# Attention of the first two layers merged with the output products of the other mixer groups

## The chip, the cores and the metric

One Trainium2 chip, one core. The metric is the device time of one launch in microseconds (us); three runs of the kernel before stand beside one profiled execution.

## The reference, cut to what matters

Four transformer layers over 256 tokens of width 1024 in float32, each modulated by a condition vector. The first two ("mix" layers) are touched by the change:

```python
def mixer_block(h, ...):
    (a_h, a_b, a_c, n_q, n_kv, n_g, l_q, l_k, l_v, l_g, l_lr, m_u, m_v) = split_cols(h @ w_in, SPLIT_SIZES)
    outs = jnp.stack([
        short_conv_mixer(a_h, a_b, a_c, conv_w),                       # group 0
        nsa_mixer(n_q, n_kv, n_g, positions, cmp_pos, cmp_w1, cmp_w2),  # group 1
        gla_mixer(l_q, l_k, l_v, l_g, l_lr, gla_gate_w2, gla_gate_b),   # group 2
        gmlp_mixer(m_u, m_v, gmlp_ws, gmlp_b),                          # group 3
    ], axis=2)
    outs = rms_norm(outs, grp_gain.reshape(N_MIXERS, GROUP_WIDTH))
    return outs.reshape(B, S, D_MODEL) @ w_o

mod = cond @ w_mod[l] + b_mod[l]
sh1, sc1, gt1, sh2, sc2, gt2 = split(mod, 6)
x = x + gt1 * rms_norm(mixer_block(rms_norm(x, g0) * (1 + sc1) + sh1, ...), g1)
x = x + gt2 * rms_norm(square(relu(h @ w_up)) @ w_down, g3)
```

Each group is 256 wide, and the norm over a group ends in one factor per token and group. `nsa_mixer` compresses keys and values (a product with `cmp_w1`), forms scores against compressed, selected and windowed keys, takes three softmaxes, and adds the three results with sigmoid gates. Layer 2 is a hybrid of a delta rule and stick-breaking attention, layer 3 retention; their arithmetic isn't touched.

## The kernel before, in words

All weights come as one stream of 1 MB slots (`pack_stream`, in the order that `plan` writes by hand) through a ring of six; the SP queue loads slot n when slot n-6 has been used (`load_weights`). A weight slot is split into a high and a low float32r part: ScalarE copies the high part (`split_hi`, L417), VectorE subtracts it (`split_lo`, L424), into two buffers used in turn. Each tile of a product is then three matmuls, high by high, low by high and high by low; a slot is 48 matmuls of 256 columns, in two halves with a semaphore each. A modulation slot isn't multiplied on TensorE: VectorE reduces it against the condition vector (`mod_sums`, L435), 4 slots for one of the 24 modulation vectors. `mods_beside` and `merge` spread these slots between the weight slots of a phase, and VectorE takes both kinds strictly in stream order.

A mix layer runs through these phases:

- `gemm_phase` ("proj", L529): 12 slots of the input product, 4 PSUM banks in turn. Each engine's program calls the next piece of a generator from `short_mixers` after each slot (`piece`), and what is left after the last (`rest`): the gated linear attention, the gated MLP and the short convolution run beside the products. The slots of the attention's inputs (q, keys, values and gates) are the last three, 9 to 11.
- `nsa_phase` (L1205 to L1457), in a block of its own, with all engines meeting before and after it: GpSimd clears the compression operand (L1239), VectorE adds positions to it (L1251) and rotates q and k (L1254 to L1264); TensorE turns q, multiplies the two compression slots (L1354), turns the rotated q and k, then computes scores (L1371, L1385), VectorE scales and masks them (L1296) and takes the row maxima, ScalarE takes the exponentials (L1451), TensorE turns the probabilities (L1410) and multiplies by the values (L1418); VectorE combines the three branches and TensorE turns the result.
- `group_norm_phase` (L1461 to L1502): squares of all four groups on ScalarE, their sums over features by a ones matrix with 512 columns (L1488), which gives the rows spread over all partitions, then Ln and Exp of [128, 1024] on ScalarE (L1476, L1482), and eight VectorE operations (L1500).
- `rows_gemm_phase` ("out", L812): 4 slots of the output product. GpSimd splits the activations into high and low parts (`split_acts`, L755 and L757). In layer 0 the 4 slots of modulation vector 4 stand between the weight slots. The last slot runs tile by tile, with sums of squares between (L601), and the norms of the next phase follow (L609, L636, L644).
- "up" and "down" of the feed-forward part.

The block of layer 0 ends its out phase with the loads of the second condition vector and of the constants of layers 2 and 3 (`later_inputs`, L2182 to L2184).

## Time and profile before

| what | us |
|---|---|
| three runs: median, lowest, highest | 1677.92, 1675.04, 5094.15 |
| profiled execution, its own time | 1681.13 |
| its span, first to last instruction | 1679.4 |
| TensorE matmul busy in it | 1529.5 |
| VectorE, ScalarE, GpSimd busy | 1106.8, 757.7, 397.8 |
| HBM read | 333.83 MB, 199 GB/s over the span |

A row of a timeline has the start and duration in us, the engine, the line of the kernel, the operation, output<-input, shapes and count; in brackets the idle time of the engine before it and what ended that. Several matmul records may be missing from a trace, so that a count can be a little short.

### The profile page before, as it was taken

Reading aid. Unit: us, or ns where it says so; the run is one execution under the profiler, and the core shown is the slowest. Engines: PE = TensorE matmul, PEld = TensorE weight load, DVE = VectorE, ACT = ScalarE, POOL = GpSimd, SP = SyncE. Lnnn points to the kernel's source line nnn. Section 1 sums busy time; section 2 is a strip of 40 time slices with the busy share of each in tenths; the row PEclk is TensorE's granted clock in tenths of the full one; section 3 lists DMA queues with packets and bytes.
Section 4 is the critical chain, followed back from the end, with each engine's and each line's share of the span. In section 5 each row is a group of like instructions: output and inputs, shape, how many; then the busy total and the mean of one; then the engine's idle time right before and its main releaser. Section 6 shows DMA issues by size and latency. Waiting matters only on the chain. (4 is left out here: it accounts for less than half of the span.)

```text
span 1679.4 us, 28072 instructions
## 1 busy us (share of the span) xinstructions
PE 1529.5 (91%) x11950; PEld 1489.0 (89%) x11950; DVE 1106.8 (66%) x1491; ACT 757.7 (45%) x1016; POOL 397.8 (24%) x369
## 2 busy tenths in 40 slices
PE   3898689999898689999899787999999998999998
PEld 3886579999887489999899687999999996999998
DVE  7874758699455549779675655777449763556554
ACT  3533445533562536543487323444335443344432
POOL 0000302099000022069200212200227800401022
PEclk7997769999799779999799897999999999989999
DMA  9760549789241127879454002577546771536550
GB/s 394 305 226 1 188 170 372 301 317 345 100 170 55 75 101 273 343 289 344 156 192 160 1 1 100 199 296 291 218 151 253 274 284 68 189 139 238 213 201 26
DMA packets 47213, 336.69 MB, mean 200 GB/s; under 512 B 5361, under 2 KB 5745, under 8 KB 6769
## 3 DMA queue, kind: packets, MB, share of 16 engines
q1 hardware_dynamic: 46224, 333.03, 53.1%
q8 instruction: 94, 1.54, 0.3%
q10 hardware_dynamic: 864, 1.87, 0.3%
q14 instruction: 31, 0.25, 0.0%
HBM read 333.83 MB, written 1.05 MB: 199 GB/s over the span
## 5 line engine op out<-in xcount | busy, mean ns | idle before, releaser
L424 DVE TENSOR_TENSOR weights_hi_lo<-ring,weights_hi_lo 128x1024 fp32r<-128x1024 f32 x426 | 554.8, 1325 | 299.1 <-ACT weights_hi_lo L417 297.9
L417 ACT ACTIVATE weights_hi_lo<-ring 128x1024 fp32r<-128x1024 f32 x426 | 445.7, 1058 | 545.9 <-PE PS L529 295.0
L529 PE MATMUL PS<-hi,weights_hi_lo 128*128 128x256 f32 x3200 | 522.8, 286 | 19.0 <-ACT hi L644 12.1
L529 PEld LDWEIGHTS PS<-hi,weights_hi_lo 128*128 128x128 f32 x3200 | 448.0, 194 | 21.5 <-issue 19.4
L812 PE MATMUL PS<-acts_hi_lo,weights_hi_lo 128*128 128x256 f32 x3552 | 437.6, 286 | 22.4 <-DVE weights_hi_lo L424 11.6
L812 PEld LDWEIGHTS PS<-acts_hi_lo,weights_hi_lo 128*128 128x128 f32 x3552 | 433.5, 193 | 26.8 <-POOL acts_hi_lo L757 14.3
L755 POOL CAST acts_hi_lo<-arena 128x256 fp32r<-128x256 f32 x148 | 133.2, 900 | 843.3 <-PE PS L812 424.6
L529 PE MATMUL PS<-lo,weights_hi_lo 128*128 128x256 f32 x1600 | 325.0, 285 | 0.0
L435 DVE CUSTOM_DVE_ANT_0 ring<-ring,cond 128x1024 f32<-128x1024 f32 x192 | 256.4, 1374 | 0.0
L529 PEld LDWEIGHTS PS<-lo,weights_hi_lo 128*128 128x128 f32 x1600 | 251.7, 193 | 0.0
L529 PE MATMUL PS<-weights_hi_lo,hi 128*128 128x256 f32 x1248 | 203.7, 285 | 3.5 <-DVE weights_hi_lo L424 2.2
L757 POOL TENSOR_TENSOR acts_hi_lo<-arena,acts_hi_lo 128x256 fp32r<-128x256 f32 x148 | 177.3, 1198 | 11.8
L529 PEld LDWEIGHTS PS<-weights_hi_lo,hi 128*128 128x128 f32 x1248 | 173.9, 191 | 5.8 <-issue 5.6
L529 PE MATMUL PS<-weights_hi_lo,lo 128*128 128x256 f32 x624 | 126.3, 284 | 0.0
L529 PEld LDWEIGHTS PS<-weights_hi_lo,lo 128*128 128x128 f32 x624 | 97.4, 190 | 0.0
L601 PEld LDWEIGHTS PS<-constS,arena 128*128 128x128 f32 x384 | 62.8, 254 | 12.3 <-ACT arena L636 11.4
L601 PE MATMUL PS<-constS,arena 128*128 128x1 f32 x384 | 63.0, 292 | 10.6 <-ACT arena L636 9.9
L1987 POOL TENSOR_TENSOR arena<-arena,constS 128x1024 f32<-128x1024 f32 x6 | 12.3, 2062 | 148.8 <-DVE arena L1915 138.8
L644 ACT ACTIVATE hi<-spare,mods 128x256 fp32r<-128x256 f32 x64 | 31.7, 506 | 32.3 <-DVE spare L655 32.3
L405 PE MATMUL PS<-constS,arena 128*128 128x128 f32 x120 | 19.7, 321 | 27.5 <-DVE arena L1336 7.6
L405 PEld LDWEIGHTS PS<-constS,arena 128*128 128x128 f32 x120 | 16.5, 167 | 30.0 <-issue 9.7
L636 ACT ACTIVATE arena<-X 128x512 f32<-128x512 f32 (+1 forms) x40 | 21.7, 545 | 43.8 <-PE PS L601 20.7
(339 smaller groups left out, 1084.5 us busy)
## 6 DMA issues: line engine op xcount, KB each, us to landing
ring<-in_stream_dram SPq DMA_DIRECT2D x313, 1024.0 KB, 4.9
constS<-in_const_dram SPq DMA_DIRECT2D x1, 1856.0 KB, 11.9
cond<-in_rows_dram SPq DMA_DIRECT2D x2, 512.0 KB, 6.0
arena<-in_x_dram ACTq DMA_DIRECT2D x1, 1024.0 KB, 12.1
smallS<-in_small_dram SPq DMA_DIRECT2D x1, 883.0 KB, 12.8
out_dram<-arena ACTq DMA_DIRECT2D x2, 256.0 KB, 2.4
out_dram<-arena SPq DMA_DIRECT2D x2, 256.0 KB, 2.8
constS<-in_const_dram SPq DMA_DIRECT2D x1, 320.0 KB, 14.1
```

What stands on the lines that cost most here:

```text
L405: mm = pe.transpose(PS[:, bank0 + i // 4, i % 4 * P:(i % 4 + 1) * P], src_of(i), ident)
L417: act.activation(wsp[:, g % 2, 0, at:at + HALF], ring[:, n % RING, at:at + HALF], ACT.Copy).then_inc(*ready.one())
L424: dve.tensor_tensor(wsp[:, g % 2, 1, at:at + HALF], ring[:, n % RING, at:at + HALF], wsp[:, g % 2, 0, at:at + HALF].bitcast(F32), ALU.subt ...
L435: ins = dve.tensor_tensor_reduce(w[:, r, :], w[:, r, :], cond[:, 0 if q < 12 else 1, :], 1.0, 0.0, ALU.mult, ALU.add, mods[:, q, k:k + 1])
L529: mm = pe.matmul(o, lhs, rhs, start=k + g + j == 0, stop=k == KD - 1 and j == 2, skip_group_check=True)
L601: mm = pe.matmul(PS[:, bank, m:m + 1], sq[:, u % 2, c * SEQ + m * P:c * SEQ + (m + 1) * P], ones[:, 0:1], start=u + c + m == 0, stop=u == ...
L636: act.activation(sq[:, u % 2, 0:len(tiles) * SEQ], X[:, tiles[0]:tiles[-1] + 1, :].rearrange("p k t -> p (k t)"), ACT.Square).then_inc(*xs ...
L644: act.activation(hi[:, k, :], tmp[:, k % 4, :], ACT.Identity, bias=mods[:, q, k:k + 1]).then_inc(*hd.one())
L755: pool.tensor_copy(asp[:, a % 2, 0, g, :], src).then_inc(*acts_hi.one())
L757: pool.tensor_tensor(asp[:, a % 2, 1, g, :], src, asp[:, a % 2, 0, g, :].bitcast(F32), ALU.subtract).then_inc(*acts_lo.one())
L812: mm = pe.matmul(y_of(k), w[:, g, k * P:(k + 1) * P], x[:, g, :], start=i + g + j == 0 and (k % 2 == 0 or k == KD - 1), stop=i == last and ...
L1987: pool.tensor_tensor(CT[v % 2], LT, cst(f"level{v}").unsqueeze(1).broadcast_to((P, 8, P)), ALU.mult).then_inc(*ctd.one())
```

## The change

1. Order of the 12 input slots: q and the keys move from places 9 and 10 to 4 and 5; mu, lg, ah, ac, ab move back to 6 to 10. The two compression slots are put into the proj phase, behind slots 4 and 5.
2. `nsa_inputs`: clearing, position adds and rotation run on GpSimd, the compression product, turning of q and of the rotated q and k on TensorE and their copies on ScalarE, all as pieces beside the proj slots (`side_by_side` calls the pieces of both generators). Proj has 3 PSUM banks in turn. The pieces of `short_mixers` stand one or two slots earlier, the convolution last.
3. `nsa_out_phase` replaces `nsa_phase` and `group_norm_phase`: phase "mixed" has three of the four output slots (groups 2, 3, 0 in that order, rows 4, 6, 0 of w_o), and the last one (group 1, the attention's) is left to "out". Score tiles rotate over banks 3 to 7; the order of scores, turns, products and sums is written by hand. The first output slot runs between the first and the second half of the turning of probabilities, the other two after the attention's products.
4. The group norms take the sum of squares with one column (`ones[:, 0:1]`) into [128, 2] per group, take the root and reciprocal of those narrow columns, and spread them by `spread_group` into PSUM; groups 2, 3 and 0 together, group 1 at the end.
5. In layer 0 the four modulation slots of vector 4 stand in the mixed phase, after the first output slot.
6. No separate blocks in layers 0 and 1. The constants of layers 2 and 3 are loaded in layer 1 (their room holds q, k and probabilities until then), behind a wait for the attention's products; the second condition vector at the end of layer 0.

```diff
-        groups = (("lk", "lr"), ("kc", "vc", "lq"), ("mv",), ("lv",), ("mu",), ("lg",), ("ah",), ("ac",), ("ab",),
-                  ("q",), ("ks", "ks", "kw", "kw"), ("vs", "vw", "ng"))
+        groups = (("lk", "lr"), ("kc", "vc", "lq"), ("mv",), ("lv",), ("q",), ("ks", "ks", "kw", "kw"), ("mu",), ("lg",),
+                  ("ah",), ("ac",), ("ab",), ("vs", "vw", "ng"))
...
+            proj[at[5] + 1:at[5] + 1] = [("cmp", ("cmp", l, 1))]
+            proj[at[4] + 1:at[4] + 1] = [("cmp", ("cmp", l, 0))]
...
+            first, others = merge(outs[:1], ("mixed", l)), [("gemm", s) for s in outs[1:3]]
+            phases.append((("mixed", l), first + [("mod", s) for q in mods_beside(("mixed", l)) for s in mod_slots(q)] + others))
+            outs = outs[3:]
...
+                gemm_phase(blk, ("proj", l), token_major, evac, banks=3, split_weights=True,
+                           beside=(side_by_side(pe, nsa_pe), side_by_side(act, nsa_act), dve, pool))
...
         # TensorE, nsa_out_phase
+                pe.wait_ge(*grc.at(1))
+                spread_group(0, 2, 0, True)
+                spread_group(1, 2, 256, False)
+                turn_probs(1)
+                pe.wait_ge(*sd.at(1))
+                turn_probs(2)
+                pe.wait_ge(*wt.at(8))
+                for g in range(2):
+                    rows_half(pe, slots[0], g, y_of, fresh=True)
...
+                attend(0, 0)
+                pe.wait_ge(*on.at(6))
+                attend(1, 2)
+                rows_half(pe, slots[1], 0, y_of, fresh=False)
+                pe.wait_ge(*fin.at(1))
+                transposes(pe, lambda i: O[:, i % 2, i // 2 * P:i // 2 * P + P], 4, 3, ft)
+                rows_half(pe, slots[1], 1, y_of, fresh=False)
+                rows_half(pe, slots[2], 0, y_of, fresh=False)
+                sums(3, 0, 0, True).then_inc(*gsum.one())
+                rows_half(pe, slots[2], 1, y_of, fresh=False)
+                pe.wait_ge(*grc.at(2))
+                spread_group(3, 2, 0, True)
...
         # VectorE, nsa_out_phase
+                normed(2, 2, 0)
+                for what, n, q, kk in todo:
+                    if what == "mod":
+                        mod_sums(dve, order, n, q, kk)
+                dve.wait_ge(*ready["gate"])
...
+                split_lo(dve, slots[1])
...
+                split_lo(dve, slots[2])
+                dve.wait_ge(*ft.at(1))
+                dve.tensor_copy(oT[:, 2:4, :], PS[:, 3, :].rearrange("p (k t) -> p k t", k=2)).then_inc(*nt.one())
+                dve.wait_ge(*grt.at(2))
+                dve.reciprocal(gr[:, 6:8], gr[:, 6:8]).then_inc(*grc.one())
                 for n in following:
                     split_lo(dve, n)
+                normed(3, 2, 0)
```

## Rows read from the trace of the kernel before

**Rows 1.** The profile's busy time, share of the span and count of TensorE.
```profile
PE 1529.5 (91%) x11950; PEld 1489.0 (89%) x11950; DVE 1106.8 (66%) x1491; ACT 757.7 (45%) x1016; POOL 397.8 (24%) x369
```

**Rows 2.** Stretches: busy us (count) of each engine, granted clock, DMA share, GB/s.
```profile
36.00:124.00 88.00, 82.60 (x636) 79.67 (x635) 69.09 (x118) 43.66 (x59) 4.47 (x6) 0.95 0.73 282
124.00:178.00 54.00, 39.20 (x229) 33.46 (x229) 26.16 (x60) 15.23 (x47) 0.95 (x1) 0.68 0.00 1
...
442.00:528.00 86.00, 81.44 (x636) 78.52 (x636) 50.76 (x83) 46.23 (x62) 4.25 (x6) 0.97 0.39 135
528.00:577.00 49.00, 33.61 (x229) 29.65 (x229) 25.98 (x60) 15.47 (x48) 0.95 (x1) 0.79 0.00 1
```

**Rows 3.** Timeline of TensorE, layer 0, from the end of proj to out.
```profile
122.73 1.04 PE L405 MATMUL PS<-constS,arena 128*128 128x128 f32 x8
127.30 1.08 PE L405 MATMUL PS<-constS,arena 128*128 128x128 f32 x4 [3.53 <-PEq L2198]
130.46 9.96 PE L1354 MATMUL PS<-ring,spare 128*32 128x128 f32 x64 [2.08 <-DVE spare L1251]
...
161.43 10.47 PE L1418 MATMUL PS<-arena 128*128 128x64 f32 x48 [0.84 <-ACT arena L1455]
...
188.83 19.73 PE L812 MATMUL PS<-acts_hi_lo,weights_hi_lo 128*128 128x256 f32 x144 [5.24 <-POOL acts_hi_lo L757]
212.19 5.46 PE L812 MATMUL PS<-acts_hi_lo,weights_hi_lo 128*128 128x256 f32 x24 [3.63 <-DVE weights_hi_lo L424]
...
223.32 1.24 PE L601 MATMUL PS<-constS,arena 128*128 128x1 f32 x8
```

**Rows 4.** The same in layer 1: end of proj, and end of out.
```profile
526.54 1.03 PE L405 MATMUL PS<-constS,arena 128*128 128x128 f32 x8
...
615.69 1.24 PE L601 MATMUL PS<-constS,arena 128*128 128x1 f32 x8
```

**Rows 5.** Timeline of TensorE in the two proj phases: where it waits.
```profile
68.78 0.71 PE L529 MATMUL PS<-weights_hi_lo,hi 128*128 128x256 f32 x4 [1.15 <-DVE weights_hi_lo L424]
...
78.74 1.19 PE L529 MATMUL PS<-hi,weights_hi_lo 128*128 128x256 f32 x4 [3.97 <-DVE weights_hi_lo L424]
...
477.03 0.72 PE L529 MATMUL PS<-weights_hi_lo,hi 128*128 128x256 f32 x4 [1.08 <-DVE weights_hi_lo L424]
484.18 0.71 PE L529 MATMUL PS<-hi,weights_hi_lo 128*128 128x256 f32 x4 [1.14 <-DVE weights_hi_lo L424]
```

**Rows 6.** The chain that ended last: a stretch of unbroken slot products.
```profile
1483.31 127.60 PE PS L529 x1056
```

**Rows 7.** Groups of TensorE in 528 to 587 us (layer 1): busy us, mean ns.
```profile
L1418 PE MATMUL PS<-arena 128*128 128x64 f32 x48 | 5.5, 275 | 0.8 <-ACT arena L1455 0.8
```

**Rows 8.** Timeline of VectorE, layer 0.
```profile
44.20 1.22 DVE L435 CUSTOM_DVE_ANT_0 ring<-ring,cond 128x1024 f32<-128x1024 f32 x1
...
67.41 2.36 DVE L424 TENSOR_TENSOR weights_hi_lo<-ring,weights_hi_lo 128x1024 fp32r<-128x1024 f32 x2
...
120.90 0.69 DVE L1096 TENSOR_TENSOR arena<-arena 128x512 f32<-128x512 f32 x1
...
124.48 0.69 DVE L1104 TENSOR_TENSOR arena<-arena 128x512 f32<-128x512 f32 x1
...
146.87 3.85 DVE L1296 SCALAR_TENSOR_TENSOR arena<-PS,constS 128x512 f32<-128x512 f32 x8
...
193.14 1.75 DVE L435 CUSTOM_DVE_ANT_0 ring<-ring,cond 128x1024 f32<-128x1024 f32 x1
```

**Rows 9.** Timeline of GpSimd, layer 0, the first split of activations in out.
```profile
187.32 0.59 POOL L755 CAST acts_hi_lo<-arena 128x256 fp32r<-128x256 f32 x1 [59.11 <-DVE arena L1500]
188.00 0.78 POOL L757 TENSOR_TENSOR acts_hi_lo<-arena,acts_hi_lo 128x256 fp32r<-128x256 f32 x1
```

**Rows 10.** Timeline of ScalarE, layer 0, in the group norm.
```profile
182.24 1.28 ACT L1476 ACT_TABLE_LOAD   x1
183.53 1.27 ACT L1476 ACTIVATE arena<-PS,constS 128x512 f32<-128x512 f32 x2
```

More of the change, by code:

```diff
@@ L92, in mods_beside @@
         return [2, 3]
-    if kind == "out" and l == 0:
+    if kind == "mixed" and l == 0:
         return [4]
@@ L458, in slots_of @@
             mod, todo, seen = mods_beside(name), [], 0
+            state["cmp"] = [n0 + d for d, (what, _) in enumerate(items) if what == "cmp"]
             for d, (what, _) in enumerate(items):
+                if what == "cmp":
+                    continue
                 if what == "mod":
@@ L499, in _ @@
                 load_weights(sp)
-                if name == ("proj", 0):
-                    sp.wait_ge(sig("layer0_inputs").sem, 32)
             @blk.tensor
@@ new lines, in side_by_side, with run, nsa_views @@
+        def side_by_side(*works):
+            def run(*args):
+                left = [w(*args) for w in works]
+                while left:
+                    left = [w for w in left if next(w, STOP) is not STOP]
+                    yield
+            return run
+        def nsa_views():
+            return {"zT": later[:, 0:1024].rearrange("p (q n) -> p q n", n=32), "hid": later[:, 1024:1152],
+                    "hidT": later[:, 1152:1184].rearrange("p (j n) -> p j n", j=2), "kcT": later[:, 1184:1200],
+                    "vc": later[:, 1200:1264], "gate": later[:, 1264:1288].rearrange("p (m c) -> p m c", m=TT),
+                    "wgt": later[:, 1288:1312].rearrange("p (b a) -> p b a", b=3), "mx": later[:, 1312:1328],
+                    "sm": later[:, 1328:1344], "sc": later[:, 1344:1472].rearrange("p (a n) -> p a n", n=16),
+                    "mxc": later[:, 1472:1480], "rsc": later[:, 1480:1488],
+                    "qT": unloaded(0, 2, SEQ), "qrT": unloaded(512, 2, SEQ), "krT": unloaded(1024, 2, SEQ),
+                    "QKR": unloaded(1536, TT, 512), "turns": unloaded(2560, 2, 64)}
@@ L974, in short_mixers @@
+        def short_mixers(l, convT, lqT, lkT, lrT, LV, LG, MU, MV, oT, blocks, rotation):
             S = 8192
@@ L1502, in group_norm_phase @@
-            state["mixed"] = [on.at(k + 1) for k in range(KD)]
+                normed(3, 2, 0)
+            state["mixed"] = [on.at(7), on.at(8)]
+            state["attended"] = ob.at(2)
             close()
@@ L2191, in _, with outputs @@
                 act.activation(cond[:, 1, :], cond[:, 1, :], ACT.Silu).then_inc(*sig("cond2_ready").one())
-            @blk.sync
-            def _(sp):
-                sp.wait_ge(sig("layer2_inputs").sem, 32)
         layers = [{"mix": mix_layer, "hyb": hyb_layer, "ret": ret_layer}[kind](l) for l, kind in enumerate(LAYERS)]
+        def outputs(blk, l, mixed, **how):
+            rows_gemm_phase(blk, ("out", l), l, mixed, 0, next_norm=(l, 1), **how)
         with block() as blk:
             start_phase(blk)
-            layers[0][0](blk)
-        for l in range(len(LAYERS)):
-            _, mixers, finish, mixed = layers[l]
-            mixers()
-            with block() as blk:
-                if finish:
-                    finish(blk)
-                rows_gemm_phase(blk, ("out", l), l, mixed, 0, acts_ready=state.pop("mixed", None), next_norm=(l, 1))
-                if l == 0:
+            for l in range(2):
+                inputs, mixers, mixed = layers[l]
+                inputs(blk)
+                mixers(blk)
+                outputs(blk, l, mixed, acts_ready=state.pop("mixed"), fresh=False)
+                if l == 1:
                     later_inputs(blk)
@@ L2212, in build, with _ @@
                     second_condition(blk)
+            layers[2][0](blk)
+            @blk.sync
+            def _(sp):
+                sp.wait_ge(sig("layer2_inputs").sem, 32)
+        for l in range(2, len(LAYERS)):
+            _, mixers, mixed = layers[l]
+            mixers()
+            with block() as blk:
+                outputs(blk, l, mixed)
+                ffn_phases(blk, l)
                 if l + 1 < len(LAYERS):
```

711 lines of the change are left out of this document (417 added, 294 removed).

## The prediction

> **What bounds the kernel now.** I read the page first: TensorE is busy 91% of the span [rows 1], so the kernel is near its bound as a whole and only stages where TensorE isn't fed can give anything. The view by stretches finds them [rows 2]. In proj TensorE is busy 82.6 of 88 us (layer 0) and 81.4 of 86 us (layer 1), at clocks of 0.95 and 0.97. Right behind, in the attention block, it is busy 39.2 of 54 and 33.6 of 49 us at 0.68 and 0.79, no other engine is half busy either, and the DMA engines move nothing: a chain of short steps between engines. The timeline of TensorE then gives its length [rows 3, 4]. In layer 0 its last work of proj ends at 122.73 + 1.04 = 123.8, the output product starts at 188.8 and ends at 223.32 + 1.24 = 224.6; three slots take 19.7 us, then it waits 3.6 us for VectorE, which had the modulation slots in between. So 100.8 us from the end of proj to the end of out. In layer 1 this stretch is 527.6 to 616.9, 89.3 us. Even in proj TensorE waits where VectorE's split is late: 1.15 + 3.97 us in layer 0 and 1.08 + 1.14 in layer 1 [rows 5], all at the places where the compression slots go now.
>
> All that isn't in these two layers stays bound by TensorE as it is; the chain that ended last shows that state: 1056 matmuls in 127.60 us, 0.121 us each, so 5.8 us for a slot of 48 and 2.9 for a half [rows 6].
>
> **Part 1, proj.** It gains the 32 compression matmuls (64 records), 4 + 8 turns of q and k and some small ones. At 1.04 us for 8 records of 128 columns [rows 3] the 64 cost 8.3 us (above, 9.96 by their own row, which was in part at the low clock; below, nothing where TensorE waits anyway). The 12 turns are 1.5, the small ones 0.9. Sum 10.7. Placed behind slots 4 and 5 they cover the waits of 5.1 and 2.2 us [rows 5]. Proj ends 5.6 us later in layer 0 and 8.5 later in layer 1. The position adds and the rotation go to GpSimd, which is busy 4.5 of the 88 us [rows 2]; at 0.8 us for an operation on 256 columns [rows 9] 17 operations are 14 us, and it has the time of four slots, 23 us, before their result is asked for: hidden. Cover gone, each microsecond of it would delay slot 11. Three banks for four: ScalarE has two slots (11.6 us) to empty a bank, where a piece of its own blocks it for about 5: nothing. The work on ScalarE and VectorE beside proj stays below their free time (44 and 69 busy of 88).
>
> **Part 2, from the end of proj to the first output product: 12.2 us.** VectorE still has the convolution, 120.90 to 125.17 before, 4.3 us [rows 8], and reaches it 1.3 us before TensorE ends because turned outputs and the next slot's split stand ahead of it: 3.0. Meanwhile TensorE does four score tiles. Then square 0.8, sums 3.3, root and reciprocal 0.7, spreading 2.4 (scores and masks stand ahead on both engines), first normed row 0.6, and GpSimd 0.59 + 0.78 = 1.4 [rows 9]. The masks go at 3.85/8 = 0.5 us each [rows 8] and end about then.
>
> **Part 3, the mixed phase.** First slot 5.8, at 18.0. Sixteen turns of probabilities, eight of compressed ones, a spread and the compressed result are some 42 records of 0.13: 5.5. The values product 5.5 by layer 1's row [rows 7], 10.5 by layer 0's [rows 3]; I take 5.5, since products have been running just before: at 29.0. In layer 1 the two last slots follow without a wait: half 2.9, turn of the result 0.6, three halves 8.7, sums and spread 1.7: at 42.9. In layer 0 VectorE has the four modulation slots from 22.1 on: 8 x 1.22 [rows 8] + 0.4, gate weights 1.4, half a split 1.2, so TensorE gets its next weights at 34.9, 5.9 us late. The result needs the other half split and five combining steps of 0.7, at 39.6; with turn, three halves, sums and spread 50.6. What is queued behind the modulation slots on VectorE is thus the whole rest of the phase. But the 3.6 us wait that they make in out today goes [rows 3].
>
> **Part 4, tail and out.** Two normed rows 1.0 and two splits on GpSimd 2.8 are on the path, at a narrow norm in place of the wide one. The last slot with its sums took 12.4 us after a wait in layer 0 (212.19 to 224.56); it is 5.8 + four sums of about 1.0 at best. I take 11.1 and 10.5. New stretch: layer 0 50.6 + 3.8 + 11.1 = 65.5, layer 1 42.9 + 3.8 + 10.5 = 57.2. Saved: 100.8 - 65.5 - 5.6 = 29.7, and 89.3 - 57.2 - 8.5 = 23.6. Sum 53.3 us.
>
> **What the sum leaves out.** It has some 25 handovers per layer without their gaps, and its values are those of a fast clock. Against that, before, the same values product took 10.5 us at one clock and 5.5 at the other, 5.0 apart [rows 3, 7]. I take 3.7 us per layer for both, 7 in all: 46 us saved. On the profiled execution's 1681.1 that is 1635; it stands 3.2 above the median of the runs, so 1677.9 - 46 = 1632 us.
>
> **The moves that cost nothing.** The 2 MB of constants go from layer 0's out phase to layer 1's; the ring is full there and TensorE-bound products follow, at a DMA share below 0.8. The wait of SP for the attention's products is long met when SP comes to it; behind it stand the up slots' loads, which would stall if it were not. The second condition vector is loaded before layer 0's last norm ends. If its landing were late, ScalarE would hold the first splits of proj 1: at most a few us once.
>
> **Two rules weighed.** ScalarE goes through a table load before Ln, and the next activation starts 1.29 us after the load began [rows 10]. The Trainium skill (ScalarE: Activation LUTs, What ACT_TABLE_LOAD costs) puts a switch at 1283 ns plus a drain of about 1380, 2.66 us; with three switches on the path of each layer (gate, root, exponential) that rule takes 8 us off the gain, 1640 for 1632. The trace agrees with the first figure and shows no drain behind the load, so the sum stays. Second: one reduction takes 1.22 us with GpSimd idle and 1.75 while GpSimd splits [rows 8]. The Trainium skill (GPSIMD Engine Reference, Key points) says that GpSimd shares its SBUF interfaces with VectorE, and the trace agrees. For the change it is two-sided: 14 us more of GpSimd beside proj, at 40% on what VectorE does then, is up to 5 us per layer of VectorE time in a stage with 19 to free, and the modulation slots run after GpSimd's last split, which is why I price them at 1.22.
>
> **Rivals.** (a) *The chain keeps its length.* Scores, softmax, turns and values are handed over as before, and the products don't fill the gaps but stand in the queue ahead of links that the chain waits for. For it: every engine's order is fixed by hand, and the first output slot stands on TensorE between turns that could run. Then only what left the chain is gained: compression and turns, 123.8 to about 142 less 10.7, some 8 us a layer with the covered waits, and about 5 for norm and meetings of the engines: 26 in all, 1652. Against it: three slots, 17 us a layer, then still run inside gaps of 15 us (54 less 39.2), so some must fit. (b) *The clock.* Slower than before if TensorE stays at 1.2 GHz from the end of proj to up. Its place: both mixed phases and the last slots. Price: small matmuls of about 22 us double, four slots go from 5.8 to 10.3 each, 40 us a layer, 80 in all; 80 - 53 = 27, so 1705. It decides against the change from two thirds of these stretches at the low level on, a granted clock of about 0.67. For it: the attention block has 0.68 today in layer 0 [rows 2]. Against it: there are products in it now, and in proj the clock is 0.95. (c) *The edit does nothing where it matters*, because other work bounds the two layers: the DMA share is 0 and no engine is full there, so I give it almost nothing; it would be 1676.
>
> **Chances.** Forecast, saved between 34 and 64: 0.76. (a) with (c): 0.18. (b): 0.06, of which 0.03 is over 2%. The range reaches down to 1613, where proj hides all compression (another 12 us beyond the sum), and up to 1660, past (a). A measurement of this kernel tells about 2% from no change. Faster by over 2% (below 1644.4): 0.77; within 2%: 0.20; slower: 0.03.
>
> **What would show it.** Right: proj grows by 4 to 9 us per layer while its waits for VectorE at slots 5 and 6 are gone; end of proj to end of out is 65 to 72 us in layer 0 and 57 to 64 in layer 1; a wait of TensorE for VectorE of about 6 us behind the values product in layer 0 and none in layer 1; a granted clock over 0.8 in both mixed phases; everything from up 0 on keeps its length. Wrong: more than 15 us between the end of proj and the first output product; a clock under 0.7; waits of proj slots for banks; position adds on GpSimd that TensorE waits for.

## The result, and the profile after

The changed kernel took 1627.6 us in the median of 4 runs (1623.3 to 1631.5), for 1677.7 of the kernel before beside it: a ratio of 0.971, with a 95% interval from 0.967 to 0.974. That is 50 us less, where 46 were forecast. One of the four runs of the kernel before took 5094.15 us; times are compared by their medians. The page of the changed kernel's profiled execution, the line of busy times as in [rows 1]:

```profile
PE 1514.1 (93%) x12038; PEld 1483.2 (91%) x12038; DVE 1083.4 (67%) x1447; ACT 748.3 (46%) x1012; POOL 420.5 (26%) x403
```

There are 88 matmul records more and 15 us less time in them: less of the work ran at the low clock (1.2 GHz of 2.4), and the granted clock over the whole span is 0.943 for 0.926. The view by stretches, columns as in [rows 2]: proj, the mixed phase and out, in layer 0 and then in layer 1.

```profile
35.00:126.00 91.00, 90.58 (x717) 87.35 (x717) 71.99 (x119) 47.30 (x69) 15.79 (x24) 0.97 0.77 302
126.00:177.00 51.00, 43.80 (x340) 41.67 (x340) 39.30 (x75) 25.73 (x58) 15.97 (x12) 0.90 0.38 142
177.00:207.00 30.00, 21.38 (x120) 20.53 (x120) 9.86 (x18) 9.12 (x22) 4.04 (x4) 0.66 0.19 70
409.00:503.00 94.00, 91.35 (x717) 87.87 (x716) 52.45 (x83) 49.06 (x70) 14.55 (x24) 0.97 0.40 147
503.00:548.00 45.00, 42.60 (x340) 40.51 (x340) 30.30 (x58) 26.02 (x58) 6.64 (x13) 0.92 0.19 70
548.00:577.00 29.00, 20.15 (x121) 19.44 (x122) 10.19 (x18) 9.64 (x22) 4.02 (x4) 0.74 0.36 142
```

The reader should see three things. Proj no longer waits in layer 0 (90.6 busy of 91 us), although it now holds the compression. The stretch behind it is busy 43.8 of 51 us at a clock of 0.90, where it was 39.2 of 54 at 0.68, and three output slots are in it. And the loss that is left stands in the third row: 21 busy of 30 us at 0.66. The timeline of TensorE tells where, the one of [rows 3] after the change:

```profile
126.20 1.65 PE L1425 MATMUL PS<-constS 64*128 64x256 f32 x16 [0.58 <-ACT arena L977]
...
137.96 5.92 PE L780 MATMUL PS<-acts_hi_lo,weights_hi_lo 128*128 128x256 f32 x48 [1.02 <-DVE heads L1587]
...
149.75 3.79 PE L1445 MATMUL PS<-arena,constS 128*128 128x64 f32 x32
153.38 1.95 PE L1445 MATMUL PS<-arena,heads 128*128 128x64 f32 x16
160.40 5.46 PE L780 MATMUL PS<-acts_hi_lo,weights_hi_lo 128*128 128x256 f32 x24 [5.07 <-DVE weights_hi_lo L432]
...
181.34 5.48 PE L836 MATMUL PS<-acts_hi_lo,weights_hi_lo 128*128 128x256 f32 x24 [4.97 <-POOL acts_hi_lo L765]
...
192.18 1.24 PE L609 MATMUL PS<-constS,arena 128*128 128x1 f32 x8
```

Proj ends at 126.20 less 0.58, 125.6; out ends at 193.4. Two long waits are left, 5.1 us for VectorE behind the values product (the product of the probabilities with the values, L1445) and 5.0 us for GpSimd ahead of the last slot, and behind each the first 24 products take 5.5 us for 3: the granted clock is 0.50 behind both waits (160.4 to 165.8 us, 181.3 to 186.6 us). In layer 1 the stretch runs from 502.8 to 563.3 with one such wait, 4.96 us ahead of the last slot, whose first 24 products take 4.5 us.

### The profile page after: what moved, and what is told of

It reads as the page before. It is cut to its first block and busy times, and to the rows that moved or that the text cites. A ratio compares the mean times of both kernels' runs of the same rounds, so it can differ in the third digit from the quotient of the medians.

```text
span 1626.1 us, 28191 instructions
## 1 busy us (share of the span) xinstructions
PE 1514.1 (93%) x12038; PEld 1483.2 (91%) x12038; DVE 1083.4 (67%) x1447; ACT 748.3 (46%) x1012; POOL 420.5 (26%) x403
## 5 line engine op out<-in xcount | busy, mean ns | idle before, releaser
L537 PEld LDWEIGHTS PS<-hi,weights_hi_lo 128*128 128x128 f32 x3200 | 445.6, 193 | 18.2 <-issue 14.9
L836 PE MATMUL PS<-acts_hi_lo,weights_hi_lo 128*128 128x256 f32 x3264 | 400.2, 285 | 18.2 <-POOL acts_hi_lo L765 9.9
L763 POOL CAST acts_hi_lo<-arena 128x256 fp32r<-128x256 f32 x148 | 139.1, 940 | 837.4 <-PE PS L836 418.4
L765 POOL TENSOR_TENSOR acts_hi_lo<-arena,acts_hi_lo 128x256 fp32r<-128x256 f32 x148 | 173.5, 1172 | 11.9
L609 PEld LDWEIGHTS PS<-constS,arena 128*128 128x128 f32 x384 | 61.3, 248 | 12.6 <-ACT arena L644 11.7
L609 PE MATMUL PS<-constS,arena 128*128 128x1 f32 x384 | 61.6, 288 | 10.7 <-ACT arena L644 9.9
L2177 POOL TENSOR_TENSOR arena<-arena,constS 128x1024 f32<-128x1024 f32 x6 | 12.3, 2063 | 151.2 <-DVE arena L2105 142.3
```

Of the source, the lines that this page charges most:

```text
L537: mm = pe.matmul(o, lhs, rhs, start=k + g + j == 0, stop=k == KD - 1 and j == 2, skip_group_check=True)
L609: mm = pe.matmul(PS[:, bank, m:m + 1], sq[:, u % 2, c * SEQ + m * P:c * SEQ + (m + 1) * P], ones[:, 0:1], start=u + c + m == 0, stop=u == ...
L763: pool.tensor_copy(asp[:, a % 2, 0, g, :], src).then_inc(*acts_hi.one())
L765: pool.tensor_tensor(asp[:, a % 2, 1, g, :], src, asp[:, a % 2, 0, g, :].bitcast(F32), ALU.subtract).then_inc(*acts_lo.one())
L836: mm = pe.matmul(y_of(k), w[:, g, k * P:(k + 1) * P], x[:, g, :], start=fresh and i + g + j == 0 and (k % 2 == 0 or k == KD - 1), stop=i = ...
L2177: pool.tensor_tensor(CT[v % 2], LT, cst(f"level{v}").unsqueeze(1).broadcast_to((P, 8, P)), ALU.mult).then_inc(*ctd.one())
```

## The experiments

All are compared with the changed kernel at 1627.6 us; each ran beside the kernel before (1678.3 to 1679.8). Four undo a part of the change, one does a part alone, and the rest move or add single pieces. Each kernel has one trace; its time is the median of four or more executions. A table behind experiment 12 sets the traces side by side.

**1. All output slots behind attention.**

```diff
         # TensorE, nsa_out_phase
-                for g in range(2):
-                    rows_half(pe, slots[0], g, y_of, fresh=True)
                 turned_taken(pe, 1)
...
-                rows_half(pe, slots[1], 0, y_of, fresh=False)
...
                 spread_group(3, 2, 0, True)
+                for i in range(3):
+                    for g in range(2):
+                        rows_half(pe, slots[i], g, y_of, fresh=i == 0)
```

> The changed kernel, with the three output slots of each mixed phase moved on TensorE behind the turn, the sums and the spread of the attention's group, so that none of them stands beside the attention; the second and third are split later too. Theory overlap (the gain is mostly products that fill gaps of the attention): 3 x 5.8 = 17.4 us a layer come back, 35 in all, about 1660 us. Theory short chain (the gain is that the attention's own tail has become short and that meetings of engines are gone; the slots only use 5 to 10 us of gaps, and without them the 5 us wait ahead of the last slot goes): 2 us more in layer 0 and 3 in layer 1, about 1633.

1629.2 us (1627.3 to 1631.3), ratio 0.970 [0.968, 0.973]: 1.5 us more than with the products among the links of the chain, which the intervals don't tell from nothing. Timeline of TensorE in layer 0:

```profile
162.20 1.12 PE L413 MATMUL PS<-constS,arena 128*128 128x128 f32 x4 [4.01 <-DVE arena L1673]
164.76 1.87 PE L1453 MATMUL PS<-constS,arena 128*128 128x1 f32 x8 [1.45 <-ACT arena L1531]
167.18 1.22 PE L1459 MATMUL PS<-constS,stat 128*128 128x128 f32 x4 [0.55 <-DVE stat L1681]
168.06 18.94 PE L780 MATMUL PS<-acts_hi_lo,weights_hi_lo 128*128 128x256 f32 x144
186.84 3.00 PE L836 MATMUL PS<-acts_hi_lo,weights_hi_lo 128*128 128x256 f32 x24
```

The chain of attention still waits (4.0 and 1.5 us), but 144 products then run without a gap, the last slot too (3.0 us for 24). From the end of proj to the end of out it is 70.9 us for 67.8 in layer 0, and 67.2 for 60.5 in layer 1, where 4.4 of the 6.7 us are the values product (10.0 us for 5.6). Out of layer 1 ends 8.6 us later than in the changed kernel. The rest of the kernel, from there on, took 1054.1 us for 1062.8 at the same instructions; the granted clock between 800 and 1100 us was 0.97 for 0.93. So the products among the links are worth some 9 us in the two layers by these two traces, 1.5 us in the time, and 35 in neither. A difference of this size between two such kernels can come from the clock in layers that no edit touches, and what a stretch says and what the time says must both be read.

**2. Compression behind proj again.**

```diff
-            proj[at[5] + 1:at[5] + 1] = [("cmp", ("cmp", l, 1))]
-            proj[at[4] + 1:at[4] + 1] = [("cmp", ("cmp", l, 0))]
+            proj += [("cmp", ("cmp", l, h)) for h in range(2)]
```

(with its products, turn and copies behind the last slot on each engine)

> The changed kernel, with both compression slots behind the twelfth proj slot and the compression, its turn and its second product behind all of proj. Theory of the prediction (the compression covers the waits of TensorE for VectorE at slots 5 and 6 in proj): these waits come back, about 5 us in layer 0 and 2 in layer 1, and behind proj stand 7.3 us that proj lost, with 3 us of hand-overs, of which VectorE's convolution covers 3: +5 and +2, at most +8 and +5: 1635 to 1641. Rival (place in proj is worth little since TensorE does the same matmuls somewhere): under 3 us in all. Rival (it was the main part): over 20 us.

1640.0 us (1638.0 to 1640.7), 12.4 more. TensorE's timeline in proj and behind it:

```profile
68.40 0.73 PE L536 MATMUL PS<-weights_hi_lo,hi 128*128 128x256 f32 x4 [1.16 <-DVE weights_hi_lo L431]
...
78.36 1.19 PE L536 MATMUL PS<-weights_hi_lo,hi 128*128 128x256 f32 x4 [3.96 <-DVE weights_hi_lo L431]
...
124.47 7.17 PE L1083 MATMUL PS<-ring,later 128*32 128x128 f32 x64
```

The waits of proj [rows 5] are back, which the compression had covered, and its 64 products stand on the path with 7.2 us, four small steps behind them. Out of layer 1 ends 13.9 us later; the values product, at the low clock in this trace, is some 5 of these in layer 1.

**3. The narrow form of the group norm alone, in the kernel before.**

```diff
-                    pe.matmul(PS[:, p, :], ones, pair[:, 2 * p:2 * p + 2, :], start=True, stop=True).then_inc(*sp_.one())
+                            mm = pe.matmul(PS[:, 0, 2 * g + m:2 * g + m + 1], sq[:, g, c, m * P:(m + 1) * P], ones[:, 0:1],
+                                           start=g + c + m == 0, stop=c == 1, skip_group_check=True)
...
+                act.activation(gr, PS[:, 0, 0:8], ACT.Sqrt, bias=cst("eps"), scale=1.0 / 256).then_inc(*grt.one())
```

> The kernel before, with only its group norm narrow: sums with one column for all four groups, one root and reciprocal of [128, 8], eight spreading matmuls, for the ones matrix with 512 columns and Ln and Exp of [128, 1024]. Theory (the narrow form alone gives little; what gives is that only one group is left behind the attention): from the last squares 0.9 sums, 0.5 root and reciprocal, 2.9 spread, 0.5 row, 1.4 split against 10.7 us from the block's start to the first product with 2.2 of squares: about 2 us less per layer, 1673 to 1677. Rival (the narrow form is a main part of the gain): over 4 us per layer, below 1669.

1678.5 us, ratio 0.999 [0.997, 1.001]: nothing. Its 16 sums with one column (32 records) took 6.98 us and the 8 spreading products (16 records) 3.42, at the low clock after a wait, and the first output product started at 190.8 us for 188.8 [rows 3].

**4. The early norms undone as well.** The kernel of experiment 1, and groups 2, 3 and 0 normed together with the attention's.

```diff
-                for i in range(3):
-                    mm = sums(i, 2, 2 * i, i == 0)
...
-                spread_group(0, 2, 0, True)
-                spread_group(1, 2, 256, False)
...
+                for i in range(4):
+                    mm = sums(i, 0, 2 * i, i == 0)
...
+                spread_group(2, 3, 0, True)
+                spread_group(3, 3, 256, False)
```

> All output slots behind attention's norm, as in the run that took 1629.2 us, and also the norms of groups 2, 3 and 0 not before the attention's but together with it. If the early norms of three groups are what shortened the way from the turned result to the first product (13.1 us before, 5.9 in the run with the products last): plus 6 to 8 us per layer, 1641 to 1645 us. If the wide form of the norm and the meetings of all engines were the cost: 1630 to 1634.

1641.4 us (1640.0 to 1641.9), 12.2 more than experiment 1. From the turn of the result to the first output product it is 12.3 us for 5.9 in layer 0. But in the two traces the stretches from the end of proj to the end of out grew by 1.4 us in layer 0 and 5.0 in layer 1, out of layer 1 ends 8.1 us later, and another 5.7 us lie behind it, at the same instructions. So of the norm it is the place that pays and not its form; how much per layer is open between 4 us by the traces and 6 by the time.

**5. The rotation behind proj.**

```diff
             def rotation(pool, order):
-                pool.wait_ge(*taken.at(6))
+                pool.wait_ge(*taken.at(12))
```

(with the turns of the rotated rows and their copies behind proj)

> The changed kernel with the rotation of q and k on GpSimd, the turning of the rotated rows and their two copies moved from beside the proj slots to behind them. GpSimd takes 2.02 us for the copy and 12 steps of 0.40, 7 us, then 8 turns of 1.3 and a copy of 0.6 ahead of the first scores. If the chain of attention sets the end: plus 8 to 10 us per layer, 1644 to 1648 us. If the phase behind has slack, since its length is then set by products and modulation slots: plus 3 to 5 per layer, 1634 to 1638.

1655.3 us (1644.5 to 1655.7), 27.7 more, and 7 above the upper end of theory 1. TensorE:

```profile
131.62 1.97 PE L1091 MATMUL PS<-constS 128*128 128x128 f32 x8 [6.89 <-POOL constS L1051]
134.32 3.07 PE L1423 MATMUL PS<-constS 64*128 64x256 f32 x16 [0.73 <-issue]
137.01 2.60 PE L1474 MATMUL PS<-later,constS 64*128 64x15 f32 x16
139.55 5.28 PE L1451 MATMUL PS<-constS,arena 128*128 128x1 f32 x24
```

8.1 us of the 13.5 by which the first output product is late (151.42 for 137.96) are the wait and the turns, as worked out. The other 5.4 are the clock: behind the wait of 6.9 us TensorE was at 1.2 GHz (granted clock 0.50 from 131.6 to 144.8 us), and the scores, the compressed scores and the sums took 3.1 + 2.6 + 5.3 us for 1.7 + 1.4 + 2.8.

This run prices an idle TensorE; it doesn't put back what the change took away. In the kernel before, the rotation ran on VectorE, in 4 us, from the first of these rows to the second:

```profile
130.34 0.69 DVE L1254 COPY arena<-arena 128x1024 f32<-128x1024 f32 x1
...
134.18 0.15 DVE L1264 COPY arena<-arena 128x1 f32<-128x1 f32 x1
```

and TensorE had the compression product until 140.4 [rows 3]. Beside that it cost nothing, where GpSimd's 6.3 us behind proj have nothing beside them.

**6. The first output slot behind the values product.**

```diff
-                for g in range(2):
-                    rows_half(pe, slots[0], g, y_of, fresh=True)
                 turned_taken(pe, 1)
...
                 attend(1, 2)
+                for g in range(2):
+                    rows_half(pe, slots[0], g, y_of, fresh=True)
```

> The changed kernel, with only the first output slot of each mixed phase moved on TensorE, from among the turns of probabilities to behind the product with the values. Theory of the prediction (in layer 0 the modulation slots on VectorE keep TensorE waiting 5 us behind the values product, so there the slot would fill the wait; in layer 1 nothing waits, and its old place covered about 2 us of exponentials): -4 in layer 0, +2 in layer 1, 1624 to 1628. Rival (the slot stands ahead of links that the chain waits for): less in both layers, 1621 or below. Rival (its place covers a gap as long as the slot): +5 in layer 1, over 1629.

1634.8 us (1633.4 to 1638.2), 7.2 more, not the 1624 to 1628 of the prediction's theory but over the 1629 of the last rival: the gain in layer 0 is 0.8 us, and layer 1 loses 9.5 from proj to up. TensorE in layer 1:

```profile
521.47 1.99 PE L1510 MATMUL PS<-later,arena 15*128 15x64 f32 x16
523.39 6.48 PE L1445 MATMUL PS<-arena,constS 128*128 128x64 f32 x32
529.67 3.62 PE L1445 MATMUL PS<-arena,heads 128*128 128x64 f32 x16
```

No wait is longer than 1.2 us here. The values product took 6.48 + 3.62 us for 3.79 + 1.95: with the slot out of the way there is a run of sums, turns and small products between 505 and 530 us, and the granted clock is 0.81 to 523.4 us and 0.53 in the values product. That the slot had kept it up isn't shown: experiments 2 and 7 to 11 have the slot in its place, and the values product ran slow in both layers of each (table below). The 7.2 us are thus the price of the place together with that of a clock that may have fallen anyway.

**7. Modulation slots behind the last output slot.** The wait of 5.1 us seemed plain: eight reductions stand on VectorE ahead of the next split.

```diff
-    if kind == "mixed" and l == 0:
+    if kind == "out" and l == 0:
         return [4]
...
+        late = [("mod", s) for q in mods_beside(("out", l)) for s in mod_slots(q)]
```

> The changed kernel with the four modulation slots of layer 0 moved once more, behind the last output slot, into a stretch where VectorE stood idle for 13.5 us. Theory 1 (TensorE's 5.1 us behind the values product are these slots, queued on VectorE ahead of the next weight split): the wait goes, 4 slots of 2.45 us fit into 13.5 us of idle VectorE, 1622 to 1624 us for 1628. Theory 2 (the wait is only exchanged, because the slots then stand ahead of VectorE's part in the last slot's norm): 1628 to 1633. GpSimd's cast of 9.7 us, which ran beside eight reductions in a row, should be near 0.4 us again under both.

1626.7 us (1621.8 to 1630.5), ratio 0.969 [0.967, 0.971], for 0.971 [0.967, 0.974]: no difference that can be told. TensorE:

```profile
150.24 7.09 PE L1446 MATMUL PS<-arena,constS 128*128 128x64 f32 x32
157.12 3.62 PE L1446 MATMUL PS<-arena,heads 128*128 128x64 f32 x16
160.50 4.38 PE L781 MATMUL PS<-acts_hi_lo,weights_hi_lo 128*128 128x256 f32 x24
```

The wait is gone, and the next output slot starts at 160.50 for 160.40. The values product ran at 1.2 GHz, 7.1 + 3.6 us. It did so in experiment 8 too, where the modulation slots are in their old place (151.13 us, 7.09 + 3.62), so their move isn't what lowered the clock. Either of the two, eight reductions on VectorE or a slow values product, holds the next slot back to about the same time, and where the product is slow the reductions are hidden behind it.

**8. TensorE kept busy in its last wait.** 36 transposes whose result nothing uses.

```diff
                 spread_group(3, 2, 0, True)
+                for _ in range(36):
+                    pe.transpose(PS[:, 3, 0:P], ones, ident)
```

> The changed kernel with 36 more transposes of constants on TensorE (their result is used by nothing), which fill its wait of 5.0 us ahead of the last output slot in layers 0 and 1. Theory 1 (TensorE loses its clock because it waits there): the first 24 matmuls of the last slot take 3.0 us for 5.5, so 2.5 us less per layer there and perhaps as much in the sums that follow; minus 4 to 8 us, 1620 to 1624. Theory 2 (the clock at that place doesn't hang on this wait, or small transposes don't keep it): the last slot keeps its 5.5 us, and the transposes, 4.7 us fast and 9 slow, just fit or overrun: 1627 to 1635.

1627.7 us (1625.5 to 1631.8): nothing in the time. In the trace the step itself came out as theory 1 has it:

```profile
176.66 4.09 PE L1530 MATMUL PS<-constS 128*128 128x128 f32 x36
181.79 3.11 PE L836 MATMUL PS<-acts_hi_lo,weights_hi_lo 128*128 128x256 f32 x24 [1.04 <-POOL acts_hi_lo L765]
```

The last slot's first 24 took 3.1 us in both layers. Layer 0's up starts 1.9 us earlier, but layer 1's values product was at the low clock this time, and from proj to up it took 173.0 us for 168.0. Up to the values product the instructions of layer 0 are those of the changed kernel, and there too it was slow this time:

```profile
151.13 7.09 PE L1445 MATMUL PS<-arena,constS 128*128 128x64 f32 x32
```

The clock at this place thus differs between executions of the same instructions.

**9. VectorE held back while GpSimd splits.**

```diff
+                if not fresh:
+                    dve.wait_ge(acts_lo.sem, 2 * rows_no[slots[-1]] + 2)
                 for n in following:
                     split_lo(dve, n)
```

> The changed kernel with one wait more: VectorE begins the weight split for the up phase only when GpSimd has split the attention's activations. Theory 1 (GpSimd's cast of 1.39 and subtraction of 1.58 us are that long because VectorE's split runs beside them; alone they took 0.40 and 0.73): TensorE's wait ahead of the last slot falls from 5.0 to 3.2 us per layer, 1624 to 1625 for 1628. Theory 2 (they are long for another reason, such as what they read): 1627 to 1629, since the split has some 15 us to spare. If the split were due earlier than I read, 1630 or more.

1623.4 us (1620.4 to 1625.1), ratio 0.967 [0.965, 0.969]: 4.2 less, as theory 1 has it, though the interval overlaps that of the changed kernel. What the time alone doesn't settle the trace does. GpSimd in layer 0, first of the changed kernel and then of this one:

```profile
177.09 0.40 POOL L763 CAST acts_hi_lo<-arena 128x256 fp32r<-128x256 f32 x1 [18.50 <-DVE arena L1601]
177.56 1.58 POOL L765 TENSOR_TENSOR acts_hi_lo<-arena,acts_hi_lo 128x256 fp32r<-128x256 f32 x1
179.09 1.39 POOL L763 CAST acts_hi_lo<-arena 128x256 fp32r<-128x256 f32 x1
180.56 0.73 POOL L765 TENSOR_TENSOR acts_hi_lo<-arena,acts_hi_lo 128x256 fp32r<-128x256 f32 x1
```

```profile
177.34 0.72 POOL L765 TENSOR_TENSOR acts_hi_lo<-arena,acts_hi_lo 128x256 fp32r<-128x256 f32 x1
178.00 0.40 POOL L763 CAST acts_hi_lo<-arena 128x256 fp32r<-128x256 f32 x1
```

The cast and the subtraction that ran beside VectorE's `split_lo` were 1.39 and 1.58 us and are 0.40 and 0.72; TensorE's wait fell from 4.97 to 3.11 us, in layer 1 from 4.96 to 3.11.

**10. The three together.** The edits of 7 to 9, VectorE's wait ahead of the modulation slots.

> The three edits of the runs beside it together: modulation slots behind the last output slot, VectorE's wait ahead of them, and 36 transposes in TensorE's wait. If each is worth what its theory 1 says and they add up: minus 5, minus 3.5, minus 4 to 8 (less what the shorter wait leaves too little room for), 1613 to 1618 us. If the transposes do nothing or overrun the shorter wait: 1620 to 1624. If the time won is given back later at a lower clock, as the later layers of the runs so far differed by 8 us with the same instructions: 1624 to 1628.

1621.8 us, but from 1613.1 to 1628.4, ratio 0.967 [0.964, 0.969]: not told apart from experiment 9 alone, and not additive.

**11. A slot in the wait ahead of the last slot.** The wait could also be filled with work that is due anyway.

```diff
-                rows_half(pe, slots[2], 0, y_of, fresh=False)
                 sums(3, 0, 0, True).then_inc(*gsum.one())
-                rows_half(pe, slots[2], 1, y_of, fresh=False)
                 pe.wait_ge(*grc.at(2))
                 spread_group(3, 2, 0, True)
+                for g in range(2):
+                    rows_half(pe, slots[2], g, y_of, fresh=False)
```

(and `normed(3, 2, 0)` ahead of VectorE's split)

> The changed kernel with both halves of the third output slot moved behind the spreading of the attention's norm, where TensorE now waits 5.0 us per layer for GpSimd, and the attention's normed rows put ahead of VectorE's split for the up phase. Theory 1 (work of a slot, 5.8 us, covers GpSimd's 4.3 us, and the norm chain starts 3 us earlier because half a slot less stands ahead of its sums): the last slot starts 3.3 us earlier per layer and runs at the full clock, 2.5 us more: 1615 to 1621 us for 1628. Theory 2 (what is saved in waits comes back as a lower clock elsewhere, as with the modulation slots moved out of the way): 1624 to 1628.

1616.6 us (1615.3 to 1624.0), ratio 0.964 [0.962, 0.967], 11 less than the changed kernel. With the products among the links, against all of them behind (experiment 1), it is now 12.6 us, and 12.4 in the traces up to the end of layer 1's out, with the values product slow in both: the overlap pays where it stands in a wait.

**12. A half slot where the clock falls.** Experiment 11, experiment 7, and half of the first slot later.

```diff
-                for g in range(2):
-                    rows_half(pe, slots[0], g, y_of, fresh=True)
+                rows_half(pe, slots[0], 0, y_of, fresh=True)
                 turned_taken(pe, 1)
...
+                rows_half(pe, slots[0], 1, y_of, fresh=True)
                 turned_taken(pe, 3)
                 pe.wait_ge(*ready["gate"])
                 attend(0, 0)
```

> The run with the third output slot behind the norm (1616.6 us), with two edits more: the second half of the first output slot moved from ahead of the turning of the probabilities to right ahead of the values product, and the modulation slots of layer 0 behind the last output slot, so that VectorE isn't late again. In that run the values product ran at 1.2 GHz in both layers (7.1 + 3.6 us for 3.8 + 2.0). Theory 1 (a half slot of wide products just ahead keeps the clock up): minus 4 to 5 us per layer, 1607 to 1611 us. Theory 2 (the low stretch only moves, into the turns that now have half a slot less ahead of them): 1614 to 1619.

1604.6 us (1601.2 to 1607.9), ratio 0.955 [0.952, 0.957]: 23 less than the changed kernel, and below the range of theory 1. TensorE in layer 0 and in layer 1:

```profile
147.04 3.10 PE L781 MATMUL PS<-acts_hi_lo,weights_hi_lo 128*128 128x256 f32 x24
149.98 3.68 PE L1446 MATMUL PS<-arena,constS 128*128 128x64 f32 x32
153.50 1.95 PE L1446 MATMUL PS<-arena,heads 128*128 128x64 f32 x16
155.26 3.08 PE L781 MATMUL PS<-acts_hi_lo,weights_hi_lo 128*128 128x256 f32 x24
...
169.41 3.11 PE L837 MATMUL PS<-acts_hi_lo,weights_hi_lo 128*128 128x256 f32 x24
...
177.89 1.24 PE L610 MATMUL PS<-constS,arena 128*128 128x1 f32 x8
...
515.40 3.68 PE L1446 MATMUL PS<-arena,constS 128*128 128x64 f32 x32
518.92 1.95 PE L1446 MATMUL PS<-arena,heads 128*128 128x64 f32 x16
```

In layer 0 no wait between the first scores and the end of out is over 1.1 us, and the granted clock from 126 to 169 us is 0.96. From the end of proj to the end of out it is 53.4 us (125.75 to 179.13), for 67.8 in the changed kernel and 100.8 before. In layer 1 there are no modulation slots, so that there the half slot stands alone: its stretch took 55.1 us for 61.5 in experiment 11, and the values product, behind the same turns and small products, 5.5 us for 10.5. In layer 0 the half slot and the freed VectorE weren't tried one without the other.

**The traces side by side.** In us; one trace for each kernel, beside the median of its times. The rest is from the end of layer 1's out to the end, at the same instructions in the changed kernel and in all that are built on it.

| kernel | median time | out 0 ends | out 1 ends | rest | values product, layers 0 and 1 |
|---|---|---|---|---|---|
| before | 1677.7 | 224.6 | 616.9 | 1062.5 | 10.5, 5.5 |
| 3 | 1678.5 | 226.1 | 619.5 | 1057.7 | 10.2, 5.5 |
| changed | 1627.6 | 193.4 | 563.3 | 1062.8 | 5.6, 5.6 |
| 1 | 1629.2 | 196.5 | 572.0 | 1054.1 | 10.4, 10.0 |
| 2 | 1640.0 | 198.8 | 577.2 | 1061.8 | 10.5, 10.5 |
| 4 | 1641.4 | 197.7 | 580.1 | 1059.8 | 10.5, 10.5 |
| 5 | 1655.3 | 207.0 | 596.5 | 1057.4 | 5.6, 10.0 |
| 6 | 1634.8 | 193.1 | 571.5 | 1062.5 | 10.5, 9.9 |
| 7 | 1626.7 | 192.0 | 566.6 | 1062.2 | 10.5, 8.7 |
| 8 | 1627.7 | 191.5 | 566.3 | 1063.8 | 10.5, 10.5 |
| 9 | 1623.4 | 190.4 | 562.6 | 1060.7 | 8.8, 8.4 |
| 10 | 1621.8 | 186.7 | 562.3 | 1064.3 | 8.8, 10.5 |
| 11 | 1616.6 | 188.7 | 559.6 | 1055.1 | 10.1, 10.5 |
| 12 | 1604.6 | 179.1 | 544.7 | 1059.8 | 5.5, 5.5 |

The rest differs by up to 10 us. The values product is at the full clock in both layers of the changed kernel and of experiment 12 alone. With the first output slot where the change put it (the changed kernel, experiments 2, 5 and 7 to 11) it is so in 3 of 16 layers.

## Why the prediction was right

**Part 1.** Proj of layer 1 grew by 8.6 us, from 85.5 (442.09 to 527.57) to 94.1 (408.69 to 502.8); 8.5 were worked out. Layer 0 ended 1.8 us later and not 5.6, and grew by 2.5, less than the 4 that were named as the least; its two waits are gone as said. It began 0.7 us earlier, its granted clock is 0.97 for 0.95, which is about 2 us of 90, and some 1 us stays unexplained. The compression products take 3.68 us for a slot of 32 records. GpSimd was cheaper than priced: its small steps take 0.32 us where 0.8 was taken from a row four times as wide, and it ended at 97.9 us, where TensorE came to turn the result at 118.8.

**Part 2.** End of proj to first output product: 12.3 us in layer 0 and 13.9 in layer 1 for 12.2; in layer 1 the sums took 4.0 us for 2.8.

**Part 3.** Wait for VectorE behind the values product: 5.07 us for 5.9 in layer 0, and none in layer 1. The phase ends 50.8 us behind proj for 50.6 in layer 0 and 44.5 for 42.9 in layer 1. The choice of 5.5 us for the values product, "since products have been running just before", came out in this trace, and that was in part luck: in the seven other kernels with the same slot ahead of it, it did so in one layer of 14. In layer 0 it matters little, since the modulation slots are as long: experiment 7 took them away and the next slot started when it had before. In layer 1 it is 5 us: experiment 8 has 65.5 us for this layer's stretch, above the 64 that were named.

**Part 4.** Last slot with its sums: 12.1 and 11.1 us for 11.1 and 10.5; wait ahead of it 5.0 for a tail of 3.8. GpSimd beside VectorE is 1.86 us of that wait per layer (experiment 9), more than the 1.2 that were missing. The weighing of the rule of the Trainium skill (GPSIMD Engine Reference, Key points) on shared interfaces looked at proj and at the modulation slots, and missed this place, where it is on the path.

**The new stretch.** 67.8 and 60.5 us, inside the 65 to 72 and 57 to 64 that were named; over the sum it is 2.3 and 3.3 us, where 3.7 each were allowed. Saved in the trace: 100.8 - 67.8 - 1.8 = 31.2 and 89.3 - 60.5 - 8.6 = 20.2, together 51.4 us, and 50 in the time. The sum had 29.7 and 23.6 ahead of the allowance: layer 0 gave more, since its proj grew by less, and layer 1 less, and that the two nearly cancel is luck. What follows keeps its length behind layer 1's out (1062.8 us for 1062.5), as was named; up and down of layer 0 are 2.7 us shorter. One reading of the rows was wrong, without effect on the sum: in layer 1's attention block VectorE is more than half busy (25.98 of 49 us, [rows 2]).

**The table load.** The three switches on this path took 1.28 us each, and the exponential's activation began as its load ended (load at 132.10, activation at 133.40 us); the loads ahead of the two roots were over before their input was there. Leaving out a drain behind the load was right.

**Rival (a), wrongly priced.** It was no outcome of the change, but experiment 1 built it: the chain without any product in it. It was put at 1652 us and took 1629.2. Its price was 13 us a layer, 8 for compression and turns and 5 for norm and meetings, 26 in all. In the trace of experiment 1 layer 1 gained 13.6 us (from the end of layer 0's down to the end of out), so there the price was right. Layer 0 gained 28.1. The chain up to the first output product got 22.6 us shorter there, close to the 23 behind the price (18.2 for compression and turns, 5 for the norm). The steps that failed are "less 10.7", where proj ended 1.8 us later, and that out was left as it was: it got 7.3 us shorter, with no modulation slots between its weight slots. Another 11.7 us of that trace's gain lie in stretches that no edit touches (3.3 in up and down of layer 0, 8.4 behind layer 1's out).

So of the 50.9 us that the changed kernel's trace gained in the two layers, 41.7 came in experiment 1 without any product in the chain, and the order of the products gave 9.2 at most. The forecast was right in its stretches and in its sum, while the words against rival (a), products in the gaps of a chain, name the smaller part. What the 41.7 consist of isn't taken apart. The compression's place is worth 12.4 us in the time and the early norms 12.2 (13.9 and 8.1 in the traces); the 27.7 of the rotation are no share of the gain, since in the kernel before it cost nothing. No run puts back the meetings of all engines, of which the one ahead of the attention block left TensorE idle for 3.53 us in each layer [rows 3]. That 27.7, 12.4, 12.2 and 1.5 add up to near 50 is chance.

**Rival (b), the clock.** 0.90 and 0.92 in the mixed phases, above the 0.8 that was named; it didn't decide against the change. The price of 10.3 us for a slot at 1.2 GHz fits the 5.5 us that its first half takes behind the waits. But it was the right thing to fear: experiments 5 and 12 turn on it, the readings of 6 and 7 are blurred by it, and out still runs at 0.66 and 0.74.

## What to carry to other kernels

Take a serial preparation (here a small product and a norm) out of the chain and lay it beside a phase of wide products before you try to push products into the chain; here it gave more and was easier to price. Before you call what a run undoes a share of the gain, look whether the kernel before really paid for it. When a wait goes and the time stays, look at the clock of what ran in its place, and whether the clock was the same in other kernels with the same instructions there. Where small matmuls follow one another for long, half a slot of wide products right ahead of the longest of them can be worth more than the same half slot early (5.5 against 10.5 us here, by one pair of kernels): put the due work where TensorE would otherwise wait or run small.

## What the runs showed of the hardware

A cast on GpSimd that takes 0.40 us alone took 9.74 beside eight modulation reductions on VectorE that ran back to back, and ended when they did:

```profile
140.99 0.40 POOL L763 CAST acts_hi_lo<-arena 128x256 fp32r<-128x256 f32 x1
...
146.89 9.74 POOL L763 CAST acts_hi_lo<-arena 128x256 fp32r<-128x256 f32 x1 [4.69 <-DVE arena L1601]
```

```profile
147.14 1.21 DVE L443 CUSTOM_DVE_ANT_0 ring<-ring,cond 128x1024 f32<-128x1024 f32 x1
...
155.16 1.21 DVE L443 CUSTOM_DVE_ANT_0 ring<-ring,cond 128x1024 f32<-128x1024 f32 x1
```

VectorE's eight reductions kept their 1.21 us. The last ended at 156.37, the cast at 156.63: in this stretch GpSimd stood still while VectorE had such instructions one behind the other, although the cast by its record had begun 0.25 us before the first of them. Elsewhere both sides pay: a reduction took 1.75 us beside GpSimd's split [rows 8], and the two halves of the last `split_lo`, 2.36 us when held back in experiment 9, took 2.90 beside the cast of 1.39 and the subtraction of 1.58:

```profile
177.33 2.90 DVE L432 TENSOR_TENSOR weights_hi_lo<-ring,weights_hi_lo 128x1024 fp32r<-128x1024 f32 x2
```

The 9.74 us cost nothing here, since the result was asked for later; with the reductions moved away (experiment 7) the same cast took 0.40. The Trainium skill (GPSIMD Engine Reference, Key points) names VectorE's instructions with two SBUF inputs as those that contend for the shared interfaces. The trace agrees, since these reductions and `split_lo` both read two tensors in SBUF; it adds the size, up to a wait for a whole row of instructions.

The clock of TensorE was down behind the waits of 5 us (0.50 from 160.4 us and from 181.3 us in the changed kernel), and it also fell in a run of sums, turns and small products with no wait over 1.2 us (experiment 6, layer 1). The same instructions get the full clock in one kernel and not in the next: up to the values product of layer 0 the changed kernel and experiment 8 have the same instructions, and it took 5.6 us in one trace and 10.5 in the other. What decides it no run here shows. The stretch behind layer 1's out, the same in all kernels, differed by up to 10 us between two profiles, with the granted clock between 800 and 1100 us at 0.97 in one and 0.93 in another.
